# A two-block layer on one core: the products of a head pair over three PSUM banks, and output-unit steps between the last pair's attention steps

## The reference, cut to what matters

```
q, k, v, z_att, z_ssm, xbc, dt_raw = split(x @ w_in)
o1, o2, o3 = windowed attention of q, k, v at dilations 1, 4, 16   (16 heads of 64, 128 steps back)
y_att = rms_norm(mix of o1, o2, o3 by their log-sum-exp * silu(z_att), att_norm_g)
y_ssm = rms_norm(ssd(conv(xbc), dt) * silu(z_ssm), ssm_norm_g)
out   = concat([y_att, y_ssm]) @ w_out
x     = layer_norm(alpha * x + out, ln_g, ln_b)
```

## Time and profile before

| what | us |
|---|---|
| runs: lowest, median, highest | 1881.64, 1886.33, 1886.8 |
| the profiled execution's own time | 1888.22 |
| its span | 1886.2 |
| PE busy in the span | 1822.3 (97%) |
| DVE, ACT, POOL busy | 1177.3, 761.9, 741.1 |
| mean granted clock of PE | 0.993 |

### The profile page before, as it was taken

The page is one execution under the profiler, slowest core; times in us unless marked ns, Lnnn a source line. Parts: engine busy times, 40 slices in busy tenths (PEclk is TensorE's granted clock), DMA queues, the critical chain, the costliest instruction groups (busy, mean ns, idle before and its releaser), DMA issues.

```text
span 1886.2 us, 27428 instructions
## 1 busy us (share of the span) xinstructions
PE 1822.3 (97%) x10670; PEld 928.7 (49%) x10670; DVE 1177.3 (62%) x2298; ACT 761.9 (40%) x1432; POOL 741.1 (39%) x696
## 2 busy tenths in 40 slices
PE   8999999999999999999999989999999999999898
PEld 5434455454444556444444546544455444544543
DVE  5558789999997768124545767571444545454537
ACT  4423553444214666214222768322333344334400
POOL 0501443463831215869113310353732663350560
PEclk9999999999999999999999999999999999999899
DMA  9011111222411112232301321022110101000702
GB/s 397 2 45 39 51 46 62 84 84 94 169 45 56 68 40 96 83 130 95 134 6 69 101 90 66 35 79 95 51 46 23 46 24 46 23 23 1 268 23 89
DMA packets 32240, 142.71 MB, mean 76 GB/s; under 512 B 3344, under 2 KB 3600, under 8 KB 27888
## 3 DMA queue, kind: packets, MB, share of 16 engines
q1 hardware_dynamic: 27888, 117.41, 16.8%
q0 software_dynamic: 4224, 23.56, 3.2%
HBM read 117.82 MB, written 23.13 MB: 75 GB/s over the span
## 4 chain that ended last, share of the span: by engine, by line
PE 72%; DVE 13%; ACT 5%; DMA 3%; POOL 3%; issue 3%; SPq 0%; DVEq 0%; POOLq 0%; ACTq 0%
PE ps L1214 38%; PE ps L1679 12%; PE ps L1208 4%; DVE arena L2149 2%; DVE small L2402 2%; PE ps L1264 2%; PE ps L1290 2%; PE ps L1251 1%; DMA hT<-in_mods 1%; PE ps L1321 1%; PE ps L1492 1%; DMA W<-in_loads 1%; PE ps L1645 1%; PE ps L1327 1%; ACT small L1945 1%
## 5 line engine op out<-in xcount | busy, mean ns | idle before, releaser
L1214 PE MATMUL ps<-hT,W 128*128 128x512 bf16 x2256 | 501.4, 380 | 6.7 <-ACT arena L1764 3.2
L1214 PEld LDWEIGHTS ps<-hT,W 128*128 128x128 bf16 x2256 | 218.0, 98 | 275.2 <-issue 13.8
L868 POOL TENSOR_TENSOR W<-W 128x512 bf16<-128x512 f32 x118 | 136.6, 1194 | 283.3 <-DMA W<-in_loads 215.5
L1214 PE MATMUL ps<-W,arena 128*128 128x512 bf16 x1080 | 239.4, 380 | 0.5 <-DVE small L2149 0.5
L1843 ACT ACTIVATE arena<-arena,small 128x128 f32<-128x128 f32 (+9 forms) x192 | 114.0, 641 | 189.2 <-DVE small L2243 168.6
L1836 ACT ACTIVATE arena<-arena,small 128x128 f32<-128x128 f32 (+9 forms) x192 | 122.9, 641 | 121.2 <-DVE small L2231 92.9
L1214 PEld LDWEIGHTS ps<-W,arena 128*128 128x128 bf16 x1080 | 105.2, 98 | 129.3 <-DVE small L2149 0.7
L2402 DVE TENSOR_SCALAR_CACHE_REDUCE small<-arena,small 128x640 bf16<-128x640 f32 (+1 forms) x124 | 126.5, 1077 | 1.1
L1214 PE MATMUL ps<-arena,W 128*128 128x512 bf16 x576 | 125.0, 379 | 0.8 <-POOL arena L929 0.5
L1679 PE MATMUL ps<-arena,W 128*128 128x512 bf16 x492 | 113.0, 379 | 2.5 <-DVE arena L2857 1.3
L2857 DVE TENSOR_TENSOR arena<-ps,arena 128x512 f32<-128x512 f32 x63 | 43.6, 692 | 111.5 <-PE ps L1679 111.5
(11 more groups left out here) (385 smaller groups left out, 3195.1 us busy)
## 6 DMA issues: line engine op xcount, KB each, us to landing
W<-in_loads SPq DMA_DIRECT2D x20, 2048.0 KB, 8.5
W<-in_groups SPq DMA_DIRECT2D x51, 256.0 KB, 3.9
W<-in_loads SPq DMA_DIRECT2D x6, 1792.0 KB, 7.1
gates_scratch<-arena SPq DMA_DIRECT2D x32, 256.0 KB, 2.0
arena<-gates_scratch POOLq DMA_DIRECT2D x2, 4096.0 KB, 13.7
arena<-sums_scratch SPq DMA_DIRECT2D x16, 512.0 KB, 3.7
W<-in_mods SPq DMA_DIRECT2D x2, 2048.0 KB, 17.2
hT<-in_mods SPq DMA_DIRECT2D x2, 2048.0 KB, 21.5
```

Of the source, the lines that this page charges most:

```text
L868: last = nc.gpsimd.tensor_tensor(low(v), v, high(v), ALU.subtract)
L1214: last = mm(o, left[:, :, a], moving, start=(k == 0 and (a, b) == PRODUCTS[0]), stop=(k == steps - 1 and (a, b) == PRODUCTS[-1]))
```

## The change

- The products of a group stand in another order, and each names a bank: 0, 4, 0, 5, 4, 5, 4. The second product of a bank adds to the first's sum in PSUM or starts afresh, by a flag. The copies of products 0 and 2 are counted by `s_first` (two a group), the five adds by `s_read`, and each product waits for the one count that it needs.
- Banks 4 and 5 come from the scores: these now always use banks 2 and 3, and wait for the bias of the item before.
- Product 6 of a group moves from place 0 to place 1 of its step (3 or 7). The tanh and the gate of a pair move from step 3 and 4 to steps 4 and 5.
- The first scores of a pair no longer wait for the last sum of q; the fifth do.
- In the last pair the 16 places take 21 of the unit steps (i, k), three units, k = 0 to 6, one or two steps a place (`OPEN_STEPS`, `open_steps`, `out_steps`). Behind the attention three more units get their k = 0 to 6, then come the sum of squares (now in bank 7) and k = 7 of six units; the other ten are made whole, over six banks.
- woA0 is loaded into chunks of the ring that are free once product 91 is made, and GpSimd splits it before the rows of pair 6, not after; woA1 follows all products as before.

```diff
-BLOCK_PRODUCTS = ((A11, B11, True), (A12, B21, False), (S2, T2, True), (A21, T3, True), (A22, T4, False),
-                  (S1, T1, True), (S4, B22, False))
+BLOCK_PRODUCTS = ((A11, B11, 0, True), (S2, T2, 4, True), (A12, B21, 0, False), (A21, T3, 5, True), (S1, T1, 4, True),
+                  (A22, T4, 5, False), (S4, B22, 4, False))
+BASE_READS, SUM_READS = 2, 5
+BASE_MADE, CORNER_MADE, FAR_CORNER, SECOND_FIRST, FIRST_SECOND = range(1, 6)
+def last_loads():
+    early, late = MADE_AT["woS0"], MADE_AT["woS1"]
+    first = late[1:8] + early[0:1]
+    second = early[2:8] + [late[0], LOADED_AT["woS1"][7]]
+    LOADED_AT["woA0"], MADE_AT["woA0"] = first, early[1:2] + first[0:7]
+    LOADED_AT["woA1"], MADE_AT["woA1"] = second, first[7:8] + second[0:7]
+OPEN_UNITS = 3
+OPEN_STEPS = [(i, k) for k in range(KD - 1) for i in range(OPEN_UNITS)]
+OUT_BANKS = (0, 4, 5, 2, 3, 6)
+def open_steps(slot):
+    n = len(OPEN_STEPS)
+    return OPEN_STEPS[n * slot // 16:n * (slot + 1) // 16]
 def group_product(j, i, place):
-    if place and i % 4 == 3:
+    if not place and i % 4 == 3:
         return None
-    return PER_GROUP * (2 * (j - 1) + i // 4) + 2 * (i % 4) + place
+    return PER_GROUP * (2 * (j - 1) + i // 4) + (6 if i % 4 == 3 else 2 * (i % 4) + place)
...
                 elif LOADS[n] in ("woA0", "woA1"):
-                    sp.wait_ge(s_prod, ALL_PRODUCTS)
+                    sp.wait_ge(s_prod, ALL_PRODUCTS - (PER_GROUP if LOADS[n] == "woA0" else 0))
...
                 if j >= 1:
                     pair_done(j - 1)
+                if j == 6:
+                    split("woA0")
                 if j == 7:
...
-                    split("woA0")
                     split("woA1")
...
                     if i == 0 and j:
-                        pe.wait_ge(s_read, 2 * PER_GROUP * j)
+                        pe.wait_ge(s_first, 2 * BASE_READS * j)
+                        pe.wait_ge(s_read, SUM_READS * (2 * j - 1) + SECOND_FIRST)
                     elif i == 0:
                         pe.wait_ge(s_free, FIRST["pair0"] + 4)
-                    if n >= 2:
-                        pe.wait_ge(sems["biased"], 2 * (n - 1))
+                    elif i == 4 and j:
+                        pe.wait_ge(s_read, 2 * SUM_READS * j)
+                    if n >= 1:
+                        pe.wait_ge(sems["biased"], 2 * n)
...
             def product(p):
-                g, (left, right, first) = p // PER_GROUP, BLOCK_PRODUCTS[p % PER_GROUP]
+                g, q = p // PER_GROUP, p % PER_GROUP
+                left, right, bank, first = BLOCK_PRODUCTS[q]
                 pe.wait_ge(s_block, p + 1)
-                if p:
-                    pe.wait_ge(s_read, p)
+                if q == 0 and g:
+                    pe.wait_ge(s_first, BASE_READS * g)
+                elif q == 1 and g:
+                    pe.wait_ge(s_read, SUM_READS * g)
+                elif q == 2:
+                    pe.wait_ge(s_first, BASE_READS * g + 1)
+                elif q >= 4:
+                    pe.wait_ge(s_read, SUM_READS * g + {4: BASE_MADE, 5: CORNER_MADE, 6: FAR_CORNER}[q])
...
+            def out_steps(some):
+                for i, k in some:
+                    u = wo + i
+                    if (i, k) == (0, 0):
+                        pe.wait_ge(s_pack, SPLIT_LOADS.index("woA0") + 1)
+                        pe.wait_ge(s_first, BASE_READS * GROUPS)
+                        pe.wait_ge(s_read, SUM_READS * GROUPS)
+                        pe.wait_ge(s_alow, 12)
+                    if k >= 6 and i == 0:
+                        pe.wait_ge(s_alow, 2 * k + 2)
+                    left, right = parts(mixA[:, k, i * P:i * P + P]), planes(chunks(MADE_AT["woA0"][k], 1))
+                    for a, b in PRODUCTS:
+                        last = mm(ps[:, unit_bank(u), :], left[:, :, a], right[:, :, b], start=(k == 0 and (a, b) == PRODUCTS[0]),
+                                  stop=(k == KD - 1 and (a, b) == PRODUCTS[-1]))
+                    if k == KD - 1:
+                        last.then_inc(s_unit, 1)
             def next_pair(n, place):
                 j, i = n // 8 + 1, n % 8
                 if j < 8 and group_product(j, i, place) is not None:
                     product(group_product(j, i, place))
+                elif j == 8 and i < 8 and n < 64:
+                    out_steps(open_steps(2 * i + place))
...
-            for u in range(wo, wo + 4):
-                unit(u, 0)
+            last_open = [(i, k) for k in range(KD - 1) for i in range(OPEN_UNITS, len(OUT_BANKS))]
+            out_steps(last_open)
             pe.wait_ge(s_yacc, 7)
...
-            for u in range(wo, wo + 4):
-                unit(u, 1)
-            for u in range(wo + 4, len(UNITS)):
+            out_steps([(i, KD - 1) for i in range(len(OUT_BANKS))])
+            for u in range(wo + len(OUT_BANKS), len(UNITS)):
                 unit(u)
```

More of the change, by code:

```diff
@@ L292, in unit_bank @@
         return UNITS[u][1] % 2
+    if UNITS[u][0][:3] == "woA":
+        return OUT_BANKS[(u - FIRST["woA0"]) % len(OUT_BANKS)]
     return (u + 2) % WIDE_BANKS
@@ L1046, in make_group @@
                 link(nc.gpsimd.tensor_tensor(v[S4], v[A12], v[S2], ALU.subtract))
-                for name, _, _ in BLOCK_PRODUCTS:
+                for name, _, _, _ in BLOCK_PRODUCTS:
                     nc.gpsimd.tensor_tensor(low(v[name]), v[name], high(v[name]), ALU.subtract).then_inc(s_block, 1)
@@ L1320, in scores @@
                     for x in range(2):
-                        last = mm(ps[:, 2 + 2 * (n % 2) + x, far:window(i)], q[halves[x], i * P:(i + 1) * P],
+                        last = mm(ps[:, 2 + x, far:window(i)], q[halves[x], i * P:(i + 1) * P],
                                   k[halves[x], max(i - 1, 0) * P:(i + 1) * P], start=True, stop=True)
@@ L1326, in scores @@
                                 at_ = i * P + RUN * r
-                                last = mm(ps[RUN * r:RUN * r + RUN, 2 + 2 * (n % 2) + x, 0:far],
+                                last = mm(ps[RUN * r:RUN * r + RUN, 2 + x, 0:far],
                                           q[halves[x], at_:at_ + RUN], of_residue(k[halves[x]], r, 0, far),
@@ L1678, in product @@
                     for a, b in PRODUCTS:
-                        last = mm(ps[:, 0, :], w[:, :, a], moved(right, k, b), start=(first and k == 0 and (a, b) == PRODUCTS[0]),
+                        last = mm(ps[:, bank, :], w[:, :, a], moved(right, k, b), start=(first and k == 0 and (a, b) == PRODUCTS[0]),
                                   stop=(k == 3 and (a, b) == PRODUCTS[-1]), skip_group_check=True)
                 last.then_inc(s_prod, 1)
+            wo = FIRST["woA0"]
+            def out_steps(some):
[14 more added lines that the diff above has]
+                        last.then_inc(s_unit, 1)
             def next_pair(n, place):
@@ L2105, in next_pair @@
                 j, i = n // 8 + 1, n % 8
-                if j < 8 and i % 4 == 0:
-                    p = group_product(j, i, place)
-                    act.wait_ge(s_prod, p + 1)
-                    if not place:
-                        if n == 0:
+                if j < 8 and place == 0 and i % 4 < 2:
+                    g = 2 * (j - 1) + i // 4
+                    act.wait_ge(s_prod, PER_GROUP * g + (3 if i % 4 else 1))
+                    bank = ps[:, 0, :]
+                    if i % 4 == 0:
+                        if g:
+                            act.wait_ge(s_read, SUM_READS * g)
+                        else:
                             act.wait_ge(s_resst[0], 16 * 4)
-                        A(base, ps[:, 0, :], ACT.Copy).then_inc(s_read, 1)
-                    elif i:
-                        A(pair_q[j % 2][:, 0:512].rearrange("p (t r s) -> p t s r", t=4, r=RES),
-                          ps[:, 0, :].rearrange("p (t s r) -> p t s r", t=4, r=RES), ACT.Copy).then_inc(s_read, 1)
-                    else:
-                        A(mixA[:, j, 0:512], ps[:, 0, :], ACT.Copy).then_inc(s_read, 1)
-                if j < 8 and place == 1 and i == 3:
-                    act.wait_ge(s_read, PER_GROUP * (2 * j - 1))
+                        last = A(base, bank, ACT.Copy)
+                    elif i == 1:
+                        last = A(mixA[:, j, 0:512], bank, ACT.Copy)
+                    else:
+                        last = A(pair_q[j % 2][:, 0:512].rearrange("p (t r s) -> p t s r", t=4, r=RES),
+                                 bank.rearrange("p (t s r) -> p t s r", t=4, r=RES), ACT.Copy)
+                    last.then_inc(s_first, 1)
+                if j < 8 and place == 1 and i == 4:
+                    act.wait_ge(s_read, SUM_READS * (2 * j - 1))
+                    act.wait_ge(s_first, BASE_READS * (2 * j - 1))
                     if j >= 2:
@@ L2840, in combine @@
                 j, i = n // 8 + 1, n % 8
-                if j == 8 or i % 4 == 0:
+                if j == 8 or group_product(j, i, place) is None:
                     return
```

(37 more changed lines are left out.)

16 lines of the change are left out of this document (7 added, 9 removed).

## The result

The changed kernel takes 1852.34 us (median of 4 runs, 1851.26 to 1852.86) against 1886.57 us for the kernel before beside it: ratio 0.9822, 95% interval 0.9803 to 0.9841. One execution in experiment 4 took 2330.61 us at a mean granted clock of 0.751, and one of the kernel before 2109.74 us at 0.849; both stand outside every figure here, and so does the profile of experiment 4, which is of the first. The profiled execution spans 1850.9 us, 35.3 less than before.

The account below looks back on a forecast made before the run. TensorE bounds the kernel until the last unit: 1888.22 us profiled, less 17.3 for waits in seven pairs and 7.6 at the end, gives 1863.3, as a median 1861.4; own range 1857 to 1866, eight in ten 1853 to 1872.

Parts of the forecast that it names:

- "Removed" step: TensorE's 24 waits in six middle pairs go: 10.3 us idle plus 3.8 hidden overlap, 14.1 us; first pair 3.2.
- The product waits: Middle pairs: 18 waits of products for sums and copies in the one bank go, 4.0 + 3.3 us plus 0.16 each.
- The seventh product: Product 6 behind its step's transposes: the wait for the copy before v is turned goes, 0.5 + 0.16 us a pair.
- Nothing is late, cost 0: Earlier transposes still find rows scaled; single score banks cost 0, covered by 4.1 us of other work; bounds 0 to 1.4 a step.
- The last pair, 42.9 us at full clock: Last pair with 21 unit steps: 38.5 us of TensorE's work plus waits, 42.9 against 38.8 before, 13.7 less afterwards.
- 2.0 us of loss by the clock: Clock falls at the last chain's idle time: end gains 7.6 us instead of 9.6; bounds 6.7 to 9.6.
- Chain of the norm: Behind the last pair: VectorE needs 3.5 us after the norm's products, cover is 3.9; unit 6's bank free with 0.4 to spare.
- The split and the gate: GpSimd's moved weight split meets one VectorE gate, costing 1.2 us of the 10 in reserve; forecast sum unchanged.
- no filling: Rival: unit steps lengthen the last pair's chain instead of filling it, 7.6 us gain lost, 1869 us; chance 8%.
- a late load: Rival: first output weights late, first unit step holds TensorE; 15 us delay, 5 over, 1866 us; chance 3%.
- one pair of score banks: Rival: TensorE waits before every scores for VectorE's bias, 0.7 us an item, 44 us, 1905 us; chance 5%.

Follow-up runs that it names:

- experiment 4: Changed kernel plus four unit steps between last scores and last weighing, without the wait for the last rows: 1849.5 us (four runs), 1850.16 with the fifth.
- experiment 5: Changed kernel with every product waiting for the read-out of the one before and the seventh product back in front of the transposes: 1871.52 us.
- experiment 3: Changed kernel with the seventh product of each group back in front of the transposes: 1860.05 us.
- kernel 13: The kernel of experiment 5 with the tanh of z and the gate one step earlier again: 1876.44 us, in two groups.
- experiment 6: The kernel before with one pair of score banks in the second attention: 1885.66 us, ratio 1.0001.
- kernel 8: The kernel of experiment 4 with one unit step moved from fourth to second place of the last pair: 1848.58 us; repeated, 1849.78 us.
- kernel 2: Changed kernel with every product waiting until the product before it is read out; order, places and filled last pair kept: 1868.64 us, in two groups.
- kernel 7: The kernel of kernel 2 with four unit steps in the tail of the last pair: 1864.05 us, one group.

## Why the prediction was off in size, step by step

The mechanism held in the main: the waits that were to go went, and the filled places paid. What failed is the size of three terms, and 0.44 us a pair that I gave to the banks came from the tanh. The median came out 9.1 us below the forecast of 1861.4: 4.1 us are in the six pairs and 1.4 in the first, where the "Removed" step counted too few waits, and 3.4 are at the end, where the waits of the last pair were 1.4 too long and the 2.0 for the clock did not come.

- **The product waits** (forecast (4.0 + 3.3 + 18 x 0.16) / 6 = 1.70 us a pair). Measured 1.98: the later tanh 0.44, the banks 1.54. I had put all of it to the banks, and counted the tanh nowhere. In size the step failed at its list: I took the 18 waits that the view names and gave each a hidden 0.16, which fits. One more in each pair, 0.22 us, was in no list, only in the distance between two starts (experiment 5); the last 0.06 lie in step 0, where the same distance was 0.94 us and is 0.87.
- **The seventh product** (forecast 0.5 + 0.16). Measured 1.06 (experiment 3). This is the term that was off most for its size: the turning of v had two waits, of which the second stands in the weight loads' list alone, and 0.2 us went because the product has other neighbours. The 1.06 holds with the other edits in place. With waiting products the same move is worth 0.67 (61.67 to 61.00), since there it brings the new wait of experiment 5; the split between this term and the one above depends on that, their sum of 3.04 does not. The 0.28 of the term above and the 0.40 of this one are 0.68 a pair, the 4.1 us by which the six pairs gained more than forecast (18.2 against 14.1); the first pair adds 1.45 (62.37 us before, 62.35 in kernel 13, 61.89 in 5, 58.79 in 3, 57.72 after: the banks give most of it, 3.1, where I had 2.6 for all its product waits).
- **"Nothing is late, cost 0"** for the single pair of score banks: right, by experiment 6 and by the empty list of waits.
- **The last pair, 42.9 us at full clock.** Measured 41.5. Its waits were 3.3 us, not 4.4: the scaling 0.9 instead of 1.7, the copies 0.9 instead of 1.4, the bias 0.4 instead of 0.7, the last close 0.8 instead of 0.6, and 0.3 of issue. What is no wait was right, 38.2 us against 38.5. The kernel with all of these covered (kernel 8) gives the check: from the last pair's start to the end it is 3.4 us shorter. My account of the 38.8 us before was looser: its parts, 23.5 + 8.4 + 6, make 37.9.
- **2.0 us of loss by the clock.** Did not occur in the profile after; its granted share is 1.00 through the last pair. But it is no invention: kernel 2, with the same tail, had it in its profile at 2.9 us, and kernel 13 at 3.0 (against kernel 5). I had put at 2.0 for certain what happens in some programs and not in others. Its upper bound of 9.6 plus 1.4 from the line above is the measured 11.0.
- **Chain of the norm.** The norm's products end at 1787.4, VectorE is done with unit 0 at 1790.75, and unit 6 begins at 1791.27, 0.5 us later (forecast 0.4), without a gap:

```profile
1785.69 1.84 PE L1760 MATMUL ps<-ck,small 128*128 128x1 f32 x16
1787.39 4.04 PE L1739 MATMUL ps<-W,arena 128*128 128x512 bf16 x18
1791.27 0.81 PE L1245 MATMUL ps<-W,arena 128*128 128x512 bf16 x3
```

```profile
1790.00 0.75 DVE L2966 SCALAR_TENSOR_TENSOR arena<-ps,small,arena 128x512 f32<-128x512 f32 x1
```

- **The split and the gate.** They met, as forecast. One piece of the split took 2.02 us instead of 1.04, beside VectorE's gate, which was barely longer than before (1.27 against the 1.20 of the earlier trace rows):

```profile
1715.86 2.02 POOL L894 TENSOR_TENSOR W<-W 128x512 bf16<-128x512 f32 x1
```

```profile
1715.71 1.27 DVE L2940 SCALAR_TENSOR_TENSOR arena<-arena 128x1024 f32<-128x1024 f32 x1
```

This agrees with the rule of the Trainium skill that the forecast cited (SBUF — State Buffer, "Who interferes with whom"); here GpSimd is the one held, by 1.0 us, and the 9.6 us of reserve are what was left after it. In kernel 13 VectorE may be held as well: its gate began at 1728.08 us, inside a copy of GpSimd of 0.61 us from 1727.93, and took 1.53 us; no run separates the two.

- **The rivals.** None occurred. Each has a measured price now: no filling 9.5 us (forecast 7.6), a late load 20.4 us of waiting where it starts 29.4 us later (forecast 5 us for 15 us of delay, the same reserve of 10), one pair of score banks 0 (forecast up to 44).

## What to carry to other kernels

A list of waits shows only some of them, and names the last link, not what made it late: here a tanh ahead of two exponentials and the copy. Before costing an edit that removes waits, measure the distance between the starts of two neighbouring operations where the wait is and where it is not. Read the list of the weight loads beside that of the matmuls: here a wait inside a group of matmuls appeared as busy time in the one and as a wait in the other. And where idle time on a saturated engine is left at the end of a stage, look for independent work that has its bank free earlier than the whole group has: here four more steps in the tail were worth 2.8 us (kernel 4), and 2.4 against the faster group of kernel 2 (kernel 7).

## What the runs showed that I had not expected

- The same tail of idle places (0.9, 0.9 and 0.5 to 0.8 us) went with a granted clock of 0.50 for 6.8 us in two programs (kernels 2 and 13, times in two groups some 4 us apart) and with full clock in others (the changed kernel, kernels 3 and 5), though their instructions there are the same. Why is open.
- The kernel before has two low-clock stretches in the last pair; with the new banks and no filling only one, 1.6 us less. Why the first one goes was not tried.
